# Attention scores of a decoder layer: two heads on the two halves of TensorE's rows, one PSUM bank for each half

## What is computed

```python
A_GROUPS = ((128, 1), (512, 4), (2048, 16))   # window, dilation
# per group g, after rotary:
s = jnp.einsum('znqhd,znkhd->znhqk', qb, kb) * (dh ** -0.5)
s = jnp.where(valid, s, -jnp.inf)             # band of `window // dilation` keys behind each query
mx = jnp.max(s, axis=-1, keepdims=True)
e = jnp.exp(s - mx)
den = jnp.sum(e, axis=-1, keepdims=True)
o = jnp.einsum('znhqk,znkhd->znqhd', e / den, vb)
```

## Time and profile before

| | |
|---|---|
| runs shown (three) | 2913.02 us median, 2911.68 to 2915.34 |
| the profiled execution | 2910.29 us, span 2908.4 us (1.9 us lie around the span) |
| mixed stage | 1472.3 to 1772.4 us of the span |
| PE busy | 2752.8 us, 95% of the span |
| mean granted TensorE clock | 0.957 of 2.4 GHz |

### The profile page before, as it was taken

How to read it: one execution, slowest core, us unless ns; L and a number is a source line. 1 busy time by engine, 2 the same in 40 slices (tenths; PEclk the granted TensorE clock), 3 DMA queues, 4 the chain that set the end, 5 groups by cost and what they waited for, 6 DMA issues and landing times.

```text
span 2908.4 us, 41826 instructions
## 1 busy us (share of the span) xinstructions
PE 2752.8 (95%) x16340; PEld 2629.6 (90%) x16340; DVE 1008.0 (35%) x2047; ACT 414.8 (14%) x847; POOL 1040.6 (36%) x1588
## 2 busy tenths in 40 slices
PE   6899999999989999999979988888999999999997
PEld 5899999999989999999967774388999999999997
DVE  7322222222282111330036655552732222222226
ACT  4100000000030010001124331110310000000002
POOL 5444444444454444444200001205454444444440
PEclk9999999999999999999978877899999999999998
DMA  4111111111114322223153234543011111111101
GB/s 151 44 44 43 43 43 43 43 43 43 43 52 147 109 90 86 93 92 105 47 187 102 91 100 174 219 156 121 30 45 49 51 44 43 43 43 43 43 0 62
DMA packets 86263, 222.06 MB, mean 76 GB/s; under 512 B 10548, under 2 KB 64236, under 8 KB 71180
## 3 DMA queue, kind: packets, MB, share of 16 engines
q1 hardware_dynamic: 61528, 191.02, 19.2%
q10 hardware_dynamic: 24628, 29.50, 2.8%
HBM read 174.61 MB, written 45.89 MB: 76 GB/s over the span
## 4 chain that ended last, share of the span: by engine, by line
PE 85%; issue 6%; DVE 5%; DMA 2%; ACT 1%; POOL 1%; SPq 0%; DVEq 0%; POOLq 0%; ACTq 0%
PE ps L719 17%; PE ps L723 17%; PE ps L722 17%; PE ps L692 8%; PE ps L695 8%; PE ps L696 8%; PE ps L934 2%; PE ps L955 1%; DVE htmp L1521 1%; DVE h_lo L1529 1%; PE ps L942 1%; PE ps L893 1%; DMA raw<-stream 1%; POOL wlo L676 1%; DMA kc<-kc_in 1%
## 5 line engine op out<-in xcount | busy, mean ns | idle before, releaser
L671 POOL TENSOR_TENSOR whi<-raw,con 128x256 fp32r<-128x256 f32 x792 | 472.2, 633 | 1784.6 <-PE ps L719 1115.3
L719 PE MATMUL ps<-h_hi,whi 128*128 128x384 f32 (+1 forms) x3072 | 1011.8, 329 | 22.8 <-POOL wlo L676 14.2
L723 PE MATMUL ps<-h_hi,wlo 128*128 128x384 f32 (+1 forms) x3072 | 1008.6, 328 | 0.3 <-issue 0.3
L722 PE MATMUL ps<-h_lo,whi 128*128 128x384 f32 (+1 forms) x3072 | 1008.4, 328 | 0.0
L719 PEld LDWEIGHTS ps<-h_hi,whi 128*128 128x128 f32 x3072 | 577.7, 188 | 28.7 <-POOL wlo L676 16.2
L722 PEld LDWEIGHTS ps<-h_lo,whi 128*128 128x128 f32 x3072 | 577.7, 188 | 0.6
L723 PEld LDWEIGHTS ps<-h_hi,wlo 128*128 128x128 f32 x3072 | 577.5, 188 | 0.0
L676 POOL TENSOR_TENSOR wlo<-raw,whi 128x256 fp32r<-128x256 f32 x792 | 573.5, 761 | 0.0
L692 PE MATMUL ps<-act_hi,whi 128*128 128x384 f32 (+1 forms) x1056 | 348.1, 330 | 14.4 <-DVE x L1551 14.4
L1560 DVE TENSOR_TENSOR ps<-silu,ps 128x384 f32<-128x384 f32 x132 | 71.3, 540 | 830.4 <-PE ps L723 539.2
L695 PE MATMUL ps<-act_lo,whi 128*128 128x384 f32 (+1 forms) x1056 | 347.0, 329 | 0.0
(11 more groups left out here) (200 smaller groups left out, 2419.2 us busy)
## 6 DMA issues: line engine op xcount, KB each, us to landing
raw<-stream SPq DMA_DIRECT2D x99, 1024.0 KB, 4.9
vc<-vc_in SPq DMA_DIRECT2D x8, 1170.0 KB, 6.2
kc<-kc_in SPq DMA_DIRECT2D x8, 1152.0 KB, 9.8
zgate<-stage ACTq DMA_DIRECT2D x16, 384.0 KB, 2.5
sgate<-zgate SPq DMA_DIRECT2D x16, 384.0 KB, 3.3
zqko<-stage ACTq DMA_DIRECT2D x12, 384.0 KB, 2.5
oc<-o_att SPq DMA_DIRECT2D x8, 396.0 KB, 6.2
va_out<-sva ACTq DMA_DIRECT2D x24, 130.0 KB, 1.8
```

Source lines behind the costliest of these rows:

```text
L671: pool.tensor_tensor(whi[:, j, cut], raw[:, j, cut], con[:, C_ONES:C_ONES + 1].to_broadcast([P, SPLIT]), ALU.mult).then_inc(hi_split, 1)
L719: mm = pe.matmul(out, w_hi, h_hi[:, k, a:a + w], start=(k == 0), stop=False)
L722: pe.matmul(out, w_hi, h_lo[:, k, a:a + w], start=False, stop=False)
L723: mm = pe.matmul(out, w_lo, h_hi[:, k, a:a + w], start=False, stop=(k == KT - 1))
```

## The change

`aqk` gets 128 partitions: heads 0 and 2 of a group lie in partitions 0 to 63, heads 1 and 3 in 64 to 127. `att_scores` fills half a bank of each of two banks: bank 4 for the heads of the lower half, bank 5 for those of the upper half, and it takes the halves in turn, so that consecutive products stand on different halves of TensorE's rows. Each unit now occupies both banks, so the scores of a unit wait for the exponentials of the unit just before, and PE's order is turned: `att_turn(u)` stands ahead of `att_scores(u+1)`. The mask takes two products of 256 columns. `load_keys` issues eight transfers of half the size in place of four.

```diff
-ATT_IN = (16 * 4, 16 * 4, 16 * 8)
+ATT_IN = (16 * 8, 16 * 8, 16 * 16)
...
-        aqk = put("aqk", [HD, 2, 2, H, SEQ])
-        aq, ak = aqk[:, :, 0], aqk[:, :, 1]
+        aqk = put("aqk", [P, 2, 2, H // 2, SEQ])
...
                 for half in range(2):
-                    for dst, src in ((aq, qr), (ak, kr_out)):
-                        sp.dma_start(dst[32 * half:32 * half + 32, s],
-                                     src[g, half, :, 0:SEQ].rearrange("(h p) t -> p h t", h=H)).then_inc(att_in[s], 16)
+                    for r in range(2):
+                        rws = slice(64 * r + 32 * half, 64 * r + 32 * half + 32)
+                        for n, src in enumerate((qr, kr_out)):
+                            sp.dma_start(aqk[rws, s, n], src[g, half, :, 0:SEQ].rearrange(
+                                "(j r p) t -> r p j t", j=2, r=2)[r]).then_inc(att_in[s], 16)
...
-                if u >= 2:
-                    pe.wait_ge(p_ready, u - 1)
-                b = 4 + u % 2
+                if u >= 1:
+                    pe.wait_ge(p_ready, u)
                 mask = (amb[:, 256:384] if g == 2 else amb[:, 256 - 128 * nk:256])
-                pe.matmul(ps[:, b, :], idb[:], mask.unsqueeze(1).to_broadcast([P, nh, nk * P]), start=True, stop=False)
-                for i in range(nh):
-                    q = tokens(aq[:, s, h0 + i, :], g, blk)
-                    k = tokens(ak[:, s, h0 + i, :], g, blk - (nk - 1), nk)
-                    mm = pe.matmul(ps[:, b, i * nk * P:(i + 1) * nk * P], q, k, start=False, stop=(i == nh - 1))
+                for r in range(2):
+                    pe.matmul(ps[:, 4 + r, 0:256], idb[:], mask.unsqueeze(1).to_broadcast([P, nh // 2, nk * P]), start=True, stop=False)
+                for j in range(nh // 2):
+                    for r in range(2):
+                        rws = slice(64 * r, 64 * r + 64)
+                        q = tokens(aqk[rws, s, 0, h0 // 2 + j, :], g, blk)
+                        k = tokens(aqk[rws, s, 1, h0 // 2 + j, :], g, blk - (nk - 1), nk)
+                        mm = pe.matmul(ps[:, 4 + r, j * nk * P:(j + 1) * nk * P], q, k, start=False, stop=(j == nh // 2 - 1))
                 mm.then_inc(as_full, 1)
...
             for u in range(LEAD):
+                att_turn(u)
                 att_scores(u + 1)
-                att_turn(u)
...
+                if u < NU:
+                    att_turn(u)
                 if u + 1 < NU:
                     att_scores(u + 1)
-                if u < NU:
-                    att_turn(u)
...
-                    ins = act.activation(ap_[:, u % 2, i * wd:(i + 1) * wd], ps[:, 4 + u % 2, i * wd:(i + 1) * wd], ACT.Exp,
+                    ins = act.activation(ap_[:, u % 2, i * wd:(i + 1) * wd], ps[:, 4 + i % 2, i // 2 * wd:(i // 2 + 1) * wd], ACT.Exp,
...
-                dve.tensor_reduce(amx[:, u % 4, 0:nh], ps[:, 4 + u % 2, :].rearrange("p (h k) -> p h k", h=nh), AX.X, ALU.max,
+                dve.tensor_reduce(amx[:, u % 4, 0:nh].rearrange("p (j r) -> p r j", r=2),
+                                  ps[:, 4:6, 0:256].rearrange("p r (j k) -> p r j k", j=nh // 2), AX.X, ALU.max,
```

## The result

The changed kernel takes 2894.6 us (median of five runs, 2891.6 to 2901.1), the kernel before 2915.3 us on the same chip: a ratio of 0.9933, 95% interval 0.9917 to 0.9949, so by this ratio 19.5 us less. The profiled execution went from 2910.29 to 2891.63 us, 18.7 us less.

What follows compares the result with a forecast made beforehand. PE bounds the feed-forwards; work, waits and low clock the mixed stage. Overlap -18.6, mask +1, bank +3, steps PE does not set +7, clock -6: -13.6, rounded -14, from 2913.0 to 2899.0 us; 8-in-10 range 2887 to 2917.

Steps and rivals of the forecast that it cites:

- What bounds the kernel: PE in both feed-forward stages, untouched; in the mixed stage work, waits and 136 us at the lower clock level.
- Two streams: Score products on two halves overlap partly: a quarter saved with two heads, three eighths with four, 18.6 us together.
- my upper end: Every pair of score products runs as one, sparing 30.8 us; as the rival of more gain 2888 us, chance 15%.
- Rivals of no overlap: Mixed-stage scores: weight loads fill strided units (2908 us, 20%); no overlap (2917, 13%); changing halves empties the array (2925, 12%).
- Mask: In the 35 score units, two mask products in place of one cost 0.03 us each, 1 us in all.
- Lost bank: Behind `args`, transposes wait 0.9 us for the exponentials in one step of three heads, costing 3 us.
- Steps that PE does not set: Around `finish`, `args` and a head's ninth step, DVE and ACT end the step; 38% of 18.6 us, 7 us lost.
- Clock: In the mixed stage, 15 of 136 us at the lower level are spared, each worth 0.41 us: 6 us gained.
- upper bound of 34: Most microseconds spared at the mixed stage's lower clock level, if every PE-bound stretch gets denser: 14 us gained.
- Loads: Twelve more issues, 1.7 us more on SP for each group, cost nothing; the bytes stay the same.

Runs made afterwards that it cites:

- the order of halves: Changed kernel with both products of the lower half, then both of the upper, in units of four heads: ratio 0.9954 to the kernel before, median 2900.2 us.
- Late scores: Changed kernel with states ahead of the transposes, outputs ahead of the scores, DVE's maximum behind hidden, in step c = 7 of three heads: ratio 0.9935 to the kernel before.
- The kernel before with half of the products: Kernel before with every other head's score products left out, keeping two banks, old order and one mask: ratio 0.9939 to the kernel before, 17.8 us less.
- the added products: Changed kernel with twelve never-read bf16 products of 512 columns added in each ninth step of a head: ratio 0.9987 to the kernel before.

## Why the prediction came out as it did

The predicted 2899.0 us and the measured 2894.6 differ by 4.4 us: 14 us of gain foretold, 19.5 measured. The mechanism was right, two streams that overlap and a part of the saving lost to waits; its main term was too small. Point by point:

- **What bounds the kernel**: right. The change shows only in the mixed stage, and there as less work, more waiting and another clock.
- **Two streams**: the term that was mis-sized. It said that "if MATMULs start in order, head 1's a can start with head 0's b, but not before", a quarter and three eighths saved, 18.6 us over the units. Measured in the loop: 25.0 us of 59.9, or 42%, with pieces of 0.63 and 1.23 us where the prediction had 0.8 and 1.4. That is "all pairs overlap in full", the assumption of my upper end, though not quite a half. Most of the miss is in the units of two heads, for which a quarter was assumed. The Trainium skill, "TensorE: Matmul & The Clock Gate", section "Part 3: Packing small matmuls — row/col tiling", says both that products of different row groups run side by side and that MATMULs start strictly in program order. The first agrees with the two starts within 10 ns. The second does not fit the unit in the order of halves, whose 1.31 us are as short as the 1.30 in the written order of the change; here the measurement decides.
- **Rivals of no overlap**: all three refuted. Strided units are at 1.23, not 2.17 us, their weight loads at 1.02, not 1.95, and no price at a change of half is seen.
- **Mask**: 1 us predicted, 0.4 us measured.
- **Lost bank**: 3 us predicted. The wait behind `args` of head 1 is 0.85 us where I said 0.9, and all waits of L945 together are 3.3 us: right in place, and right in size as waiting. What it costs in time is not shown apart: bank, order and masks together are 6 us (0.6 to 11.7) without the second stream, and "Late scores", which took that wait away for head 1, gave nothing back.
- **Steps that PE does not set**: 7 us predicted, 10 with the lost bank; PE's idle time grew by 12.9 us. Right in kind: the steps c = 4 to 7 of head 1, with `args` among them, got hardly shorter (1612.46 - 1586.29 = 26.2 us before and 25.4 after), while c = 0 to 3 went from 26.4 to 21.4 us.
- **Clock**: 6 us predicted; 7.7 us are the remainder of the ledger, and the untouched lines fell by 10.6. Of the lower level 29 us were spared and not 15, near the upper bound of 34; at 0.41 us each that would be 12 us.
- **Loads**: nothing predicted, and no cost of the extra issues is seen. New are PE's waits for `ao`, 4.2 us in two, because DVE waits for a store of `ao`: 8.9 us in two waits in the mixed stage, against 0.4 us before. The longer one lies near the end of the loop, where the store stands in SP's queue behind the loads of the sample tokens, which the change leaves alone; the keys were loaded long before.

```profile
1695.68 1.37 SPq L531 DMA_DIRECT2D sks<-kr_out  x3
...
1698.59 10.48 SPq L509 DMA_DIRECT2D o_att<-ao  x4
...
1704.92 0.43 DVE L1848 COPY ao<-ps 128x260 f32<-128x260 f32 x1 [6.58 <-DMA o_att<-ao]
```

The kernel before with half of the products has four transfers, as before, and the same two waits (PE 2.4 us in two, the longer 2.2). So they need no extra issues. That they appear because PE comes to these places sooner is argued, not tried.

The sum was nearer than its main term, and that is partly luck: the overlap was 6.4 us better than assumed (25.0 against 18.6), the clock's part 1.7 and the mask 0.6, and the losses, 3 us larger (12.9 against 10), took back a part.

Open: why the clock in the loop stands at 0.85 in the changed kernel and at 0.77 to 0.81 in seven of the eight variants of it (all but the one with halves in order, 0.84).

## What to carry to other kernels

Products of 64 rows on two halves of TensorE's rows took a little under six tenths of their PE time here, also with strided operands and, in units of four heads, in either order of writing. Count the gain only in the steps that PE ends: here three fifths of PE's saving showed, and the three edits at waits behind `args` and in the ninth step gave nothing back. Before crediting or blaming an edit, follow it past its own step, to where the wait has gone and to the granted clock behind it: an edit that shortened its own step by 1 us put 1.4 us onto ACT in the next one and made the kernel before 9 us slower.

## What was not expected of the hardware

- Two products on different halves start within 10 to 30 ns, also when both products of one half are written ahead of the first of the other; units of four heads take 1.23 in place of 2.17 us.
- A step in which PE was busy for 18.84 of 18.84 us had a granted clock of 0.64; the same step without the added products, busy for 11.98 of 13.42 us, had 0.75.
- An edit on DVE and ACT alone, which shortened one step by 1 us and made PE wait 2.27 us in the next, came with a ninth step wholly at the lower level (0.50, 17.5 in place of 14.2 us).
